# A hybrid decoder block on one core: gate-up weights of experts 9 to 30 fetched as 4 MB transfers into five homes of 32 KB per partition

## What is computed

```python
logits = (hf @ w_router + b_router).astype(jnp.float32)
top_v, top_i = lax.top_k(logits, TOP_K)              # 4 of 32
gate = jax.nn.softmax(top_v, axis=-1)
...
gu = xb @ w_gu[e] + b_gu[e]                          # w_gu[e]: 1024 x 2048, 8 MB
g_lin = jnp.minimum(gu[..., :D_FF], SWIGLU_LIMIT)
u_lin = jnp.clip(gu[..., D_FF:], -SWIGLU_LIMIT, SWIGLU_LIMIT)
act = g_lin * jax.nn.sigmoid(SWIGLU_ALPHA * g_lin) * (u_lin + 1.0)
return act @ w_down[e] + b_down[e]                   # w_down[e]: 1024 x 1024, 4 MB
```

## Time and profile before

| | |
|---|---|
| median of 3 runs | 1238.6 us (1238.01 to 1238.61) |
| span of the profiled execution | 1237.7 us |
| PE busy | 1179.7 us, 95% of the span |
| DVE, ACT, POOL busy | 307.4, 230.3, 230.1 us |
| bytes moved | 451.99 MB, mean 365 GB/s |
| packets of the DMA queue of SP | 54056, 88.6% of 16 engines' span |

### The profile page before, as it was taken

The page is one execution under the profiler, slowest core; times in us unless marked ns, Lnnn a source line. Parts: engine busy times, 40 slices in busy tenths (PEclk is TensorE's granted clock), DMA queues, the critical chain, the costliest instruction groups (busy, mean ns, idle before and its releaser), DMA issues.

```text
span 1237.7 us, 13553 instructions
## 1 busy us (share of the span) xinstructions
PE 1179.7 (95%) x5931; PEld 579.5 (47%) x5931; DVE 307.4 (25%) x463; ACT 230.3 (19%) x312; POOL 230.1 (19%) x200
## 2 busy tenths in 40 slices
PE   9999999999999999999999999998999999898996
PEld 9987788988433333333333333333333333333332
DVE  5447364224411212121122112111211211121112
ACT  6473676445100000000000000000000000000001
POOL 6977759982000000000000000000000000000000
PEclk9999999999999999999999999999999999999999
DMA  9644437648999999999999999999999999999994
GB/s 315 206 136 136 170 103 244 247 164 346 406 412 415 426 429 427 427 428 428 428 428 427 428 427 429 426 428 427 427 427 428 428 429 428 426 428 428 428 427 191
DMA packets 54120, 451.99 MB, mean 365 GB/s; under 512 B 6668, under 2 KB 6760, under 8 KB 29352
## 3 DMA queue, kind: packets, MB, share of 16 engines
q1 hardware_dynamic: 54056, 451.06, 88.6%
HBM read 450.00 MB, written 1.05 MB: 364 GB/s over the span
## 4 chain that ended last, share of the span: by engine, by line
PE 62%; DMA 33%; DVE 3%; ACT 1%; issue 1%; POOL 0%; DVEq 0%; ACTq 0%; POOLq 0%
PE ps L1155 21%; DMA ring<-in_w_down 18%; PE ps L1177 11%; PE ps L778 10%; DMA spare<-in_w_down 7%; DMA kv_small<-in_w_down 7%; PE ps L723 6%; PE ps L1133 4%; PE ps L1101 2%; PE ps L1085 2%; PE ps L1197 1%; PE ps L744 1%; PE ps L802 0%; PE ps L762 0%; PE ps L890 0%
## 5 line engine op out<-in xcount | busy, mean ns | idle before, releaser
L467 POOL TENSOR_TENSOR w_parts<-ring,w_parts 128x512 fp32r<-128x512 f32 x162 | 219.3, 1389 | 45.9 <-ACT w_parts L1326 41.8
L616 POOL TENSOR_SCALAR ss<-ss 128x2 f32<-128x2 f32 (+2 forms) x7 | 1.3, 192 | 955.2 <-ACT junk L1316 950.9
L1155 PE MATMUL ps<-ring,xs 128*64 128x512 f32 x640 | 143.9, 596 | 10.5 <-DMA ring<-in_w_gu 9.7
L1994 DVE TENSOR_SCALAR xbuf<-ps 128x512 f32<-128x512 f32 x32 | 22.1, 691 | 525.1 <-PE ps L1155 525.1
L1155 PE MATMUL ps<-ring,nT 128*64 128x512 f32 x608 | 136.6, 595 | 8.7 <-DMA ring<-in_w_gu 8.7
L1177 PE MATMUL ps<-ring,xbuf 128*64 128x512 f32 x592 | 134.2, 597 | 7.4 <-DMA ring<-in_w_down 7.4
L778 PE MATMUL ps<-w_parts,xT_hi 128*128 128x512 f32 x352 | 112.1, 399 | 0.0
L1564 ACT ACTIVATE xbuf<-xbuf 128x512 f32<-128x512 f32 x32 | 20.2, 631 | 461.8 <-DVE xbuf L1994 461.8
L1155 PEld LDWEIGHTS ps<-ring,xs 128*64 128x64 f32 x640 | 43.9, 137 | 101.6 <-issue 80.9
L1326 ACT ACTIVATE w_parts<-ring 128x2048 fp32r<-128x2048 f32 x41 | 78.3, 1917 | 68.1 <-PE ps L778 42.4
L1574 ACT ACTIVATE xbuf<-ps 128x512 f32<-128x512 f32 x32 | 19.2, 599 | 371.2 <-PE ps L1197 371.2
(11 more groups left out here) (292 smaller groups left out, 1247.3 us busy)
## 6 DMA issues: line engine op xcount, KB each, us to landing
ring<-in_w_gu SPq DMA_DIRECT2D x78, 2048.0 KB, 43.2
ring<-in_w_down SPq DMA_DIRECT2D x36, 2048.0 KB, 42.8
kv_small<-in_w_gu SPq DMA_DIRECT2D x13, 2048.0 KB, 39.3
gates_xn<-in_w_gu SPq DMA_DIRECT2D x13, 2048.0 KB, 44.3
ring<-in_w_in SPq DMA_DIRECT2D x24, 1024.0 KB, 5.4
spare<-in_w_gu SPq DMA_DIRECT2D x12, 2048.0 KB, 43.7
xcq<-in_w_gu SPq DMA_DIRECT2D x11, 2048.0 KB, 44.6
xcq<-in_w_down SPq DMA_DIRECT2D x8, 2048.0 KB, 38.8
```

Source lines behind the costliest of these rows:

```text
L467: ops.tensor_tensor(w_lo[:, m % SPLIT, c], ring_slot(m)[:, c], w_hi[:, m % SPLIT, c], ALU.subtract).then_inc(lo_ready[name], 1)
L1155: i = mm(ps[64 * half:64 * half + 64, 4 + q, :], xg[:, k, (j % GE) * SLOTS:(j % GE + 1) * SLOTS], w[:, q * FF + half * 512:q * FF + half * ...
L1994: V.tensor_scalar(gl, ps[:, 4, :], LIM, None, ALU.min).then_inc(gl_ready, 1)
```

## The change

- Every expert matrix is now read with k=4: a gate-up quad is 512 rows of w_gu, four neighbouring rows (32 KB) per partition. `pair_rows`, `paired`, `wr`, `gmoe` and the transposes of h follow this order.
- The ten homes become five of 32 KB per partition, each with a lower and an upper half: three in `ring`, `kv_quad` (`kv`, `small` and all of `gates`), and `spare_quad` (`spare`, now placed ahead of `xcT`, with `xcT` and `qT` behind it). `home(m)` is a function of the pair number: quad m // 2 goes to home quad m // 2 mod 5. Pair 10 still goes to `once`; pair 11 goes to half 0 of its quad.
- `hn2` moves to `xn`, `prob` to `xbuf`, `probT` to `small`.
- Quads 25 to 91 without the down quads (`whole`) are fetched by one transfer of 4 MB with one semaphore (`fetch_quad`); that is the gate-up of experts 9 to 30. All others, the down pairs among them, are fetched in halves of 2 MB, as before.
- The first fetches are in a new order: pair 1 behind the first chunk of w_xq, then pairs 3, 4, 5, 2, 0, 6, 7 (`EARLY`), then from 10 on in their order.

The core of the diff:

```diff
-def turn(m):
-    return m if m < ONCE else m - 1
+DOWN_QUAD = dn_at(0, 0) // 2 % (EXP_PR // 2)
+EARLY = [(0, 3), (1, 0), (1, 1), (0, 2), (0, 0), (1, 2), (1, 3)]
+HALVED = 5 * QUADS
+LAST_WHOLE = MAIN_PR // 2 - 1 - 4
+def home(m):
+    return 2 * (m // 2 % QUADS) + (0 if m == ONCE + 1 else m % 2)
+def whole(quad):
+    return HALVED <= quad <= LAST_WHOLE and quad % (EXP_PR // 2) != DOWN_QUAD
+def pair_sem(m):
+    return home(m) - home(m) % 2 if whole(m // 2) else home(m)
...
 def last_user(m):
-    r = turn(m) - PAIRS
-    return r if r < ONCE else r + 1
+    return max(i for i in range(m - m % 2) if i != ONCE and (home(i) == home(m) or whole(m // 2) and
+                                                               home(i) // 2 == home(m) // 2))
...
-        hn2 = gates[:, 0, :].rearrange("p (b d) -> p b d", b=TB)
-        prob = gates[:, 0, :].rearrange("p (u m) -> p u m", m=T)
-        probT = gates[:, 1, :].rearrange("p (h m t) -> p h m t", h=H_XA, m=TB)
+        hn2 = xn
+        prob = xbuf[:, 0:TB * D].rearrange("p (u m) -> p u m", m=T)
+        probT = small[:].rearrange("p (h m t) -> p h m t", h=H_XA, m=TB)
...
         def pair_rows(t):
-            return t[:].rearrange("p b (c q k) -> p b c k q", q=P, k=2)
+            return t[:].rearrange("p b (c q k) -> p b c k q", q=P, k=4)
...
+            def gate_up_rows(e, quad):
+                src = w_gu[0, bass.ds(e, 1), quad * 4 * P:(quad + 1) * 4 * P, :]
+                return src.rearrange("e (p k) n -> p (e k) n", p=P)
             def fetch_gate_up(w, e, c, full):
-                src = w_gu[0, bass.ds(e, 1), c * 2 * P:(c + 1) * 2 * P, :]
-                sp_.dma_start(w, src.rearrange("e (p k) n -> p (e k) n", p=P)).then_inc(full, 16)
+                sp_.dma_start(w, gate_up_rows(e, c // 2)[:, 2 * (c % 2):2 * (c % 2) + 2, :]).then_inc(full, 16)
+            def fetch_quad(m, e, c):
+                sp_.dma_start(quad_home(m // 2 % QUADS), gate_up_rows(e, c // 2)).then_inc(main_full(m), 16)
...
+                if m == CHUNK_AT[(FIRST["xq"], 0)]:
+                    first_free(1)
+                    fetch_gate_up(main_pair(1), 0, 1, main_full(1))
...
-            for n in range(NE + 1):
+            for n, c in EARLY:
+                m = gu_at(n, c)
+                pair_free(m)
+                fetch_gate_up(main_pair(m), n, c, main_full(m))
+            for n in range(2, NE + 1):
                 for c in range(GU_PR):
                     if n < NE:
                         m = gu_at(n, c)
-                        pair_free(m)
-                        fetch_gate_up(main_pair(m), n, c, main_full(m))
+                        if not whole(m // 2):
+                            pair_free(m)
+                            fetch_gate_up(main_pair(m), n, c, main_full(m))
+                        elif c % 2 == 0:
+                            pair_free(m)
+                            fetch_quad(m, n, c)
...
             def h_transposes(half, b, bank):
-                for c in range(2):
-                    for k in range(2):
-                        i = nc.tensor.transpose(ps[:, bank, (2 * c + k) * P:(2 * c + k + 1) * P],
-                                                pair_rows(h)[:, b, 2 * half + c, k, :], ident[:])
+                for k in range(4):
+                    i = nc.tensor.transpose(ps[:, bank, k * P:(k + 1) * P], pair_rows(h)[:, b, half, k, :], ident[:])
```

More of the change, by code:

```diff
@@ L161, in halves_pair @@
     return (HALF_SLOT + 2 * (m % SPLIT)) // 2
-KV_SMALL, GATES_XN = RING // 2, RING // 2 + 1
-PAIR_ORDER = [1, X_SLOT // 2, KV_SMALL, halves_pair(FRONT_CH - 3), 0, GATES_XN,
-              halves_pair(FRONT_CH - 2), halves_pair(FRONT_CH - 1)]
+QUADS = 5
+RING_QUADS = RING // 4
+KV_QUAD, SPARE_QUAD = RING_QUADS, RING_QUADS + 1
+QUAD_ORDER = [KV_QUAD, 0, 1, 2, SPARE_QUAD]
 STEP_PR = BODY * EXP_PR
@@ L169 @@
 assert STEP_PR % OLD_PAIRS == 0
-assert sorted(PAIR_ORDER) == list(range(OLD_PAIRS))
+assert PAIRS == 2 * QUADS and halves_pair(FRONT_CH - 3) == 3 and halves_pair(FRONT_CH - 1) == 5
 DN_PR = EXP_PR - GU_PR
-SPARE_PR, XCQ_PR = OLD_PAIRS, OLD_PAIRS + 1
 MAIN_PR = NE * EXP_PR
@@ L191 @@
 GATHERED_IN = {n: (4 * (n - 2), 4 * (n - 2) + 2) if n in (2, 3) else (2 * (n % GE),) for n in range(2, NE - 1)}
-def turn(m):
-    return m if m < ONCE else m - 1
+DOWN_QUAD = dn_at(0, 0) // 2 % (EXP_PR // 2)
[8 more added lines that the diff above has]
+    return home(m) - home(m) % 2 if whole(m // 2) else home(m)
 def pair_filled(m):
-    return 16 if m == ONCE else 16 * (turn(m) // PAIRS + 1)
+    if m == ONCE:
+        return 16
+    return 16 * sum(i != ONCE and pair_sem(i) == pair_sem(m) and not (whole(i // 2) and i % 2)
+                    for i in range(m + 1 if not whole(m // 2) else m - m % 2 + 1))
 def last_user(m):
-    r = turn(m) - PAIRS
-    return r if r < ONCE else r + 1
+    return max(i for i in range(m - m % 2) if i != ONCE and (home(i) == home(m) or whole(m // 2) and
+                                                               home(i) // 2 == home(m) // 2))
 TR_X, TR_Y, TR_MEM, TR_MERGED, TR_H1, TR_H2 = range(6)
@@ L260, in build @@
         xbuf = sb("xbuf", [P, 3072])
+        spare_at = aligned()
+        spare = sb("spare", [P, 2, CH])
         xcT_at = aligned()
@@ L264, in build @@
         qT = sb("qT", [P, H_SB // 2, T])
-        xcq = nc.alloc_sbuf_tensor_at("xcq", [P, 2, CH], F32, offset=xcT_at)
+        spare_quad = nc.alloc_sbuf_tensor_at("spare_quad", [P, 4, CH], F32, offset=spare_at)
         aligned_of["xs"] = aligned()
@@ L273, in build @@
         xn = sb("xn", [P, TB, D])
-        kv_small = nc.alloc_sbuf_tensor_at("kv_small", [P, 2, CH], F32, offset=kv_at)
-        gates_xn = nc.alloc_sbuf_tensor_at("gates_xn", [P, 2, CH], F32, offset=gates_at + 2 * D * 4)
+        kv_quad = nc.alloc_sbuf_tensor_at("kv_quad", [P, 4, CH], F32, offset=kv_at)
         aligned_of["scr"] = aligned()
@@ L279, in build @@
         junk_t = sb("junk", [P, 2 * TB * TABW])
-        spare = sb("spare", [P, 2, CH])
         pcol = sb("pcol", [P, ROWS])
@@ L371, in pair_rows, with quad_home @@
         def pair_rows(t):
-            return t[:].rearrange("p b (c q k) -> p b c k q", q=P, k=2)
+            return t[:].rearrange("p b (c q k) -> p b c k q", q=P, k=4)
         def paired(t):
-            return t.rearrange("p b (c k q) -> p b c k q", k=2, q=P)
+            return t[:].rearrange("p b (c k q) -> p b c k q", k=4, q=P)
         def ring_slot(m):
             return ring[:, slot(m), :]
+        def quad_home(q):
+            r = QUAD_ORDER[q]
+            return {KV_QUAD: kv_quad, SPARE_QUAD: spare_quad}[r][:, :, :] if r >= RING_QUADS else \
+                ring[:, 4 * r:4 * r + 4, :]
         def pair_home(q):
[L385 to L391, removed]
+            return quad_home(q // 2)[:, 2 * (q % 2):2 * (q % 2) + 2, :]
         def main_pair(m):
-            return once[:, :, :] if m == ONCE else pair_home(turn(m) % PAIRS)
+            return once[:, :, :] if m == ONCE else pair_home(home(m))
         def main_full(m):
-            return once_in if m == ONCE else pair_full[turn(m) % PAIRS]
+            return once_in if m == ONCE else pair_full[pair_sem(m)]
         def quadrant(i):
@@ L493, in fetch_down, with first_free @@
                     sp_.dma_start(dst[:, 2:4, :], src[:, 2:4, :]).then_inc(tail, 16)
+            def first_free(q):
+                r, late = QUAD_ORDER[q // 2], q % 2
+                if r == 0:
+                    eng, count = lo_count(LAST_RAW + 1 if late else FRONT_CH - 1)
+                    sp_.wait_ge(lo_ready[eng], count)
+                elif r == 1 and not late:
+                    eng, count = lo_count(LAST_RAW + 2)
+                    sp_.wait_ge(lo_ready[eng], count)
+                    sp_.wait_ge(chunk_used, products_done(FIRST["xq"]))
+                elif r == KV_QUAD and not late:
+                    sp_.wait_ge(xa_lg, H_XA)
+                    sp_.wait_ge(chunk_used, products_done(FIRST["xv"]))
+                    sp_.wait_ge(xa_o, 2)
+                elif r == KV_QUAD:
+                    sp_.wait_ge(stripe_out["dve"], emptied(FIRST["sb_out"] + 2)[1])
+                elif r != SPARE_QUAD:
+                    sp_.wait_ge(chunk_used, next(m for m in range(FRONT_CH - SPLIT, FRONT_CH)
+                                                 if 2 * r + late == halves_pair(m)) + 1)
             sp_.dma_start(h[:], x[0].rearrange("(b p) d -> p b d", p=P)).then_inc(x_in, 16)
@@ L514, in _ @@
                 if m == RING_SPLIT + 1:
[L515 to L518, removed]
+                    sp_.dma_start(wr[:].rearrange("p (c k) n -> p c k n", k=4),
+                                  w_router[0].rearrange("(c p k) n -> p c k n", p=P, k=4)).then_inc(late_in, 16)
+                    sp_.dma_start(gmoe[:].rearrange("p (c k) -> p c k", k=4),
+                                  g_moe[0].rearrange("(c p k) -> p c k", p=P, k=4)).then_inc(late_in, 16)
```

(10 more changed lines are left out.)

## The result

The changed kernel takes 1240.15 us in the median of 21 runs (1239.46 to 1241.05) against 1238.21 us (1237.71 to 1238.89) of 21 runs of before: ratio 1.0016, 95% interval 1.0010 to 1.0021. It is 1.9 us slower, inside the 0.2% that was called "same". The forecast was 1240.3.

What follows compares the result with a forecast made beforehand. The prediction took the DMA stream of weights to bound the kernel. Lost turn +4.1, larger transfers -2.8 and strides +0.4 make +1.7 us on the span of 1237.7, plus 0.9 around it: 1240.3 us, range 1235.8 to 1245.0.

Steps and rivals of the forecast that it cites:

- The bound: End of the expert phase: the DMA stream, never pausing from 350 us on, sets the end, plus 24.8 us of compute.
- Part 1: Start of the expert stream: pair 12 and later ones wait one use longer for homes; +3.3 to +4.9 us, 4.1 taken.
- start-up pauses of before: Pauses among pairs 12 to 15 in the earlier kernel, 0 to 1.6 us, deducted from the lost turn's 4.9 us.
- Part 2: Gate-up weights of experts 9 to 30: 44 transfers of 4 MB save packets; -0.3 to -4.0 us, 2.8 taken.
- two-point line: Packet time against packet size, from two full-queue stretches of the earlier trace: 5.7 ns per packet beyond its bytes.
- rival (a): Faster: long runs also move their bytes faster; whole quads 1.6% faster would save 7.0 us, giving 1236.1; chance 0.14.
- (c): Slower: 32 KB runs are cut to 16 KB, the larger transfers save only 0.3 us, giving 1242.8; chance 0.08.
- (b): Slower: engines reading 32 KB rows in step share parts of memory; 4.3 us per 1% of rate lost; chance 0.12.
- Rival (d): Each queued transfer has a start of its own that landings don't show; 44 fewer would give 1120 us; chance 0.01.
- Part 3: TensorE waits for whole quads, and they are issued only when both home halves are used; cost 0, without cover 3.5 us.
- the cover: TensorE's idle time before the last three landings, 3.7 us in all, said to absorb its falling behind by up to 3.5.
- Part 4: Router path before the experts: stride 16 B slows the h transposes, 0 to +2.2 us, 0.4 taken; copies to hn2 covered.

## Why the prediction was right, and where it was not

**The bound** was read rightly: every kernel here ends by the stream, and what was put into its start or its rate came out at the end (for the router's 0.7 us alone this isn't shown, see above). (The level of 426 to 429 GB/s begins with the fourteenth slice of the earlier trace rows, not with the twelfth; nothing hangs on it.)

**Part 1, the turn**: forecast +3.3 to +4.9 us, 4.1 taken. Shown by the kernels without it: 4.84 us by the medians, beside whole quads and beside halves, and 4.9 us by the bytes that are missing in the first 20 us. The mechanism, the pair and the issue times were right. The top of the range was the right value: of the 0 to 1.6 us that were taken off for start-up pauses of before nothing shows in these bytes.

**Part 2, the transfers**: forecast -0.3 to -4.0, 2.8 taken; 3.4 measured by the medians, 3.55 by B. The term was a little small because a packet costs about 9 ns and not the 5.7 of the two-point line through the fast stretch of the earlier trace rows. The slower stretch there, which gives 8.5, was the better row. Behind 700 no slice is above 432 GB/s, the sign that was named for rival (a), and the packets' price accounts for the rise, so it falls; 32 KB runs are neither cut (c) nor slowed by their pitch (b): after's rate rose. Rival (d), a start per transfer, falls with the packets' price, which accounts for the whole.

**Part 1 and 2 together** were forecast at +1.3 us; B rose from 893.87 and 894.16 to 895.22 and 894.83, by 1.0 us in the means.

**Part 3, the coarse waits**: forecast 0; measured 0.03 us by the medians, which can't be told from 0. But the cover is thinner than thought. TensorE's last idle time before the end, 1.16 us in the earlier trace rows, is 0.37 us after, because its clock fell in the whole quad before and 1.7 us went there:

```profile
1174.28 8.78 PE L1192 MATMUL ps<-kv_quad,nT 128*64 128x512 f32 x32 [2.43 <-DMA kv_quad<-in_w_gu]
1213.43 3.65 PE L1214 MATMUL ps<-spare_quad,xbuf 128*64 128x512 f32 x16 [0.37 <-DMA spare_quad<-in_w_down]
```

**Part 4, the strides**: the size was about right (+0.4 forecast, +0.7 by A), and that was luck, since the step was wrong. The transposes, for which it was taken, cost nothing: their loads take 212 ns with 16 B against 209. The copy to `hn2`, which was called covered because it ends before the first gather, doubled, and who waited was not the gather but the exponentials queued behind it on ScalarE. What is queued behind a lengthened instruction on its engine had to be followed, not only its own reader. The Trainium skill (SBUF — State Buffer, Door 1: The DMA port swizzle) describes lines of 16 bytes in SBUF, of which an access pattern should hit each at least twice for full speed; a stride of 16 B in float32 hits each once, one of 8 B twice. ScalarE's 2.15 us against 1.22 agree with that. TensorE's loads don't: they pay at 8 B (209 ns against 140 for contiguous h) and nothing more at 16 B (212).

**The sum**: +4.8 for the turn, -3.4 for the transfers and +0.5 for the rest are the 1.9 measured, by the medians. By the marks, +1.0 us of stream and +0.7 of router make 1.7. That the forecast came within 0.2 us of the time is partly luck: the turn was taken 0.7 us too small and the saving 0.6 too small, and the before that it was added to (1238.6) lies 0.4 us above the 1238.21 it was compared with. The forecast took 0.9 us around the span; each run that lists both has 1.7, and the profiled span of before was about 1.2 us long, most of it by the multiplication above. As the sum was made on the median, this did no harm. The 0.2 us between 1.7 and 1.9 aren't explained, nor are they beyond what the marks vary by.

## What to carry to other kernels

Where a stream of transfers sets the end, each of its pauses is paid in full unless the bytes were loaded before (the first pause here), and a home that stands empty costs one transfer's time with nothing queued (pair 12) and nothing where 3.3 pairs are queued (pair 50): do realignments and coarser units there, not at the start. A larger run saves about 9 ns per packet saved, here 3.4 us of 1240, and is easily lost to one turn of the buffers. When an access pattern's stride changes, look at what is queued behind the instruction on its engine.

## What the runs showed of the hardware

- **TensorE's clock** falls behind some of the waits for a whole quad, and not behind others of the same length. Before, the granted clock was 1.00 in every stretch shown, with waits of at most 1.33 us between the pairs of expert 31. After, twelve quads behind 600 come behind a wait of 2.4 to 2.7 us; seven of them take 8.5 to 8.8 us and five 7.09. What decides between them isn't shown. One of the slow ones: the stretch 1086.6 to 1090.0 has 0.57, which is nearly the whole of it at 1.2 GHz, behind 2.65 us of idle time, and the quad takes 8.51 us where others take 7.09. It is back at 2.4 GHz behind it. The kernel with coarse waits alone has eight such quads. The rows show that slow quad and one at 7.09 us.

```profile
1086.63 8.51 PE L1192 MATMUL ps<-ring,xs 128*64 128x512 f32 x32 [2.65 <-DMA ring<-in_w_gu]
...
1145.07 7.09 PE L1192 MATMUL ps<-ring,nT 128*64 128x512 f32 x32 [2.42 <-DMA ring<-in_w_gu]
```
```profile
1086.60:1090.00 3.40, 3.37 (x10) 1.15 (x12) 0.00 (x0) 0.00 (x0) 0.00 (x0) 0.57 1.07 458
1090.00:1100.00 10.00, 10.00 (x46) 3.90 (x44) 3.88 (x6) 0.63 (x1) 0.00 (x0) 1.00 1.01 433
```

- **A ScalarE copy** of 128 x 1024 float32 takes 2.15 us with a source stride of 16 B and 1.22 with 8 B.
- **A data packet** costs about 9 ns beyond its bytes (8.7 to 9.5 by the accounts above), from 8 to 16 KB runs and from 16 to 32 KB alike, in a queue that is full.
- **One VectorE multiplication** beside GpSimd work took 2.36 us in one execution and 1.22 in another of the same kernel. Whether the GpSimd work decides it was not tried.
